# A two-layer encoder with 32 experts on one core: the first expert's two blocks by halves of its rows, the buffer refilled by halves, a pick moved behind them, and six added products ahead of the ranks

## The reference, cut to what matters

```
def route(xt, w_router, router_bias):
    scores = sigmoid(xt @ w_router); biased = scores + router_bias
    g_sel = argmax(sum of the 2 highest biased scores of each group)
    masked = where(in_group(g_sel), biased, -inf)
    _, idx = lax.top_k(masked, 2)
    w = take_along_axis(scores, idx); return idx, w / sum(w)

def expert(xb, e):                       # 32 experts, each for the tokens that chose it
    g, u = split(xb @ w_gu[e], 2, axis=-1)
    return (silu(g) * u) @ w_dn[e]

for i in range(2):
    x = x + g1 * mixer[i](modulate(x, norm_mix[i], sh1, sc1))
    h = modulate(x, norm_ffn[i], sh2, sc2)
    x = x + g2 * sum over k of w[:, k] * expert(h, idx[:, k])
```

## Time and profile before

| | |
|---|---|
| median of 3 runs | 1720.48 us (1718.47 to 1720.78) |
| profiled execution, its own time | 1716.08 us |
| its span, first to last instruction | 1714.3 us |
| mean granted TensorE clock | 0.904 |
| PE busy | 1363.5 us, 80% |
| DVE, ACT, POOL busy | 40%, 21%, 17% |
| moved by DMA | 517.29 MB, mean 302 GB/s |
| the chain that ended last | PE 50%, DMA 37%, DVE 8% |

### The profile page before, as it was taken

The page is one execution under the profiler, slowest core; times in us unless marked ns, Lnnn a source line. Parts: engine busy times, 40 slices in busy tenths (PEclk is TensorE's granted clock), DMA queues, the critical chain, the costliest instruction groups (busy, mean ns, idle before and its releaser), DMA issues.

```text
span 1714.3 us, 33172 instructions
## 1 busy us (share of the span) xinstructions
PE 1363.5 (80%) x14067; PEld 742.5 (43%) x14067; DVE 688.5 (40%) x1322; ACT 356.2 (21%) x717; POOL 298.8 (17%) x340
## 2 busy tenths in 40 slices
PE   3999899898956758797746999797986767698854
PEld 3644455444534334364424444344543334364432
DVE  5676677667311102121205378656531112022113
ACT  3345565221100001010002144523110001011000
POOL 1001122000312122132100122200131123122200
PEclk9998999998978879899977999898997889899987
DMA  9651422499999999999997122047799999999997
GB/s 367 242 217 69 164 75 77 142 321 404 380 391 401 406 387 386 405 389 410 412 417 286 49 74 74 24 171 320 290 397 397 405 405 386 402 389 401 420 426 292
DMA packets 66841, 517.29 MB, mean 302 GB/s; under 512 B 13277, under 2 KB 26102, under 8 KB 49034
## 3 DMA queue, kind: packets, MB, share of 16 engines
q1 hardware_dynamic: 51696, 493.77, 72.7%
q0 software_dynamic: 10848, 16.24, 2.8%
q10 hardware_dynamic: 4154, 5.18, 0.9%
HBM read 506.27 MB, written 22.04 MB: 308 GB/s over the span
## 4 chain that ended last, share of the span: by engine, by line
PE 50%; DMA 37%; DVE 8%; ACT 2%; issue 2%; SPq 1%; PEldq 1%; POOL 0%; ACTq 0%; DVEq 0%; POOLq 0%
DMA ring_gu<-in_moe_w_gu_dram 31%; PE ps L1188 15%; PE ps L1195 6%; PE ps L1078 6%; DMA ring_gu<-in_w_ada_dram 4%; PE ps L1113 3%; PE ps L995 3%; PE ps L1097 2%; PE ps L908 2%; PE ps L969 2%; PE ps L1015 2%; PE ps L888 2%; DMA arena<-xn_dram,tok_idx 2%; PE ps L1137 2%; PE ps L935 2%
## 5 line engine op out<-in xcount | busy, mean ns | idle before, releaser
L1188 PE MATMUL ps<-ring_gu,arena 128*32 128x256 f32 x5248 | 350.5, 423 | 173.6 <-DMA ring_gu<-in_moe_w_gu_dram 159.2
L1188 PEld LDWEIGHTS ps<-ring_gu,arena 128*32 128x32 f32 x5248 | 182.7, 121 | 323.2 <-issue 124.4
L2087 DVE TENSOR_TENSOR arena<-arena,ps 128x128 f32<-128x128 f32 x120 | 34.5, 287 | 631.5 <-ACT arena L1611 631.4
L719 POOL DMA_INDIRECT ys_dram<-arena,out_idx x116 | 114.7, 989 | 659.8 <-DVE arena L2081 618.8
L1611 ACT ACTIVATE arena<-ps 128x128 f32<-128x128 f32 x120 | 33.3, 278 | 886.8 <-PE ps L1188 886.8
L1188 PE MATMUL ps<-arena 128*32 128x256 f32 x2432 | 153.5, 409 | 61.5 <-DMA arena<-in_moe_w_gu_dram 58.3
L1195 PE MATMUL ps<-ring_dn,arena 128*32 128x256 f32 x2624 | 155.9, 379 | 2.8 <-DVE arena L2092 2.8
L712 POOL DMA_INDIRECT arena<-xn_dram,tok_idx x104 | 95.8, 922 | 278.4 <-issue 151.3
L1188 PEld LDWEIGHTS ps<-arena 128*32 128x32 f32 x2432 | 81.9, 118 | 127.2 <-DMA arena<-in_moe_w_gu_dram 53.5
L1195 PEld LDWEIGHTS ps<-ring_dn,arena 128*32 128x32 f32 x2624 | 84.4, 110 | 61.3 <-DVE arena L2092 3.7
L1078 PE MATMUL ps<-arena 128*128 128x512 f32 x256 | 110.6, 592 | 0.2 <-ACT arena L1325 0.2
(11 more groups left out here) (360 smaller groups left out, 1551.9 us busy)
## 6 DMA issues: line engine op xcount, KB each, us to landing
ring_gu<-in_moe_w_gu_dram SPq DMA_DIRECT2D x44, 4096.0 KB, 31.8
ring_dn<-in_moe_w_dn_dram SPq DMA_DIRECT2D x43, 2048.0 KB, 28.8
arena<-in_moe_w_gu_dram SPq DMA_DIRECT2D x18, 4096.0 KB
arena<-in_moe_w_dn_dram SPq DMA_DIRECT2D x20, 2048.0 KB, 28.8
ring_gu<-in_w_ada_dram SPq DMA_DIRECT2D x12, 2048.0 KB, 20.3
ring_gu<-in_w_ada_dram SPq DMA_DIRECT2D x48, 512.0 KB, 4.9
ring_gu<-ys_dram SPq DMA_DIRECT2D x8, 1024.0 KB, 9.5
arena<-in_rnn_w_in_dram SPq DMA_DIRECT2D x8, 1024.0 KB, 6.9
```

The costliest lines, as they stand in the source:

```text
L719: g.indirect_dma_start(ys_dram, bass.IndirectOffsetOnAxis(ap=out_idx[:, col:col + 1], axis=0), yo[:, n % 4, :], None, bounds_check=2 * TIL ...
L1188: last = mm(ps[s_ * ROWS:(s_ + 1) * ROWS, pb, 0:2 * QF].rearrange("p (a b) -> p a b", a=2), rows[:, k, :], pair[:, :, s_, :], start=(k == ...
```

## The change

Four edits.

1. Blocks 0 and 1, PE. Before, block 0's eight steps were followed by block 1's eight. Now the first four steps of block 0, the first four of block 1 (then the new semaphore `gu_half`), the last four of block 0, the last four of block 1. The down product of block 0 follows as before.
2. The load of place 3 (expert 3 into the buffer of expert 0), SP. Before, one DMA of 4 MB after block 1's product. Now two of 2 MB: the first half of each partition's row after `gu_half`, the second after block 1's product. `gu_landed` counts the additional 16.
3. `pick_rows(1, 0)` on PE moves from before block 0 to after block 2 and the down product of block 1; its copy `picks_out(1, 0)` on ACT moves from before block 0's Silu to before block 3's.
4. Ahead of the wait for `chosen_ready`, PE makes `KEEP_BUSY` = 6 products of 128x512 from `ident` and `x_tok` into the bank that the ranks overwrite. Nothing reads them.

A fifth edit: the semaphore `mrow_in` is merged into `rows_in` at the kernel's start.

```
@@ -473,7 +474,8 @@
         def gu_landed(place, l):
-            return landed(place, l) + (16 * (FT + l) if place % RING == RING - 1 else 0)
+            pieces = {0: l + (place >= RING), 1: 0, RING - 1: FT + l}
+            return landed(place, l) + 16 * pieces[place % RING]
@@ -585,8 +587,13 @@
                 def load_expert(n):
                     o = ORDER[n]
                     e = o if n < FIXED else sp.value_load(order_i[o:o + 1, 0:1], min_val=0, max_val=NE - 1)
+                    rows = GU[n % RING].rearrange("p k n -> p (k n)")
+                    half = KT * HALF if n == RING else 0
+                    if half:
+                        sp.wait_ge(S["gu_half"], l + 1)
+                        sp.dma_start(rows[:, 0:half], gu_rows(l, e)[:, 0:half]).then_inc(S["gu_in0"], 16)
                     sp.wait_ge(S["gu_done"], gone(n - RING, l))
-                    sp.dma_start(GU[n % RING].rearrange("p k n -> p (k n)"), gu_rows(l, e)).then_inc(S[f"gu_in{n % RING}"], 16)
+                    sp.dma_start(rows[:, half:KT * D], gu_rows(l, e)[:, half:KT * D]).then_inc(S[f"gu_in{n % RING}"], 16)
                     sp.wait_ge(S["dn_done"], gone(n - RING, l))
@@ -1116,8 +1122,11 @@
+                g = STAGES[f"rank{l}"]
+                pe.wait_ge(*emptied(before_in_bank(g + 1)))
+                for _n in range(KEEP_BUSY):
+                    mm(bank(g + 1), ident[:, :], x_tok[:, 0, 0:HALF], start=True, stop=True)
                 pe.wait_ge(S["chosen_ready"], l + 1)
-                g = STAGES[f"rank{l}"]
@@ -1153,7 +1162,6 @@
                 picks_transposed(0)
-                pick_rows(1, 0)
@@ -1248,7 +1256,13 @@
                     mine_rows = xgT[:, t % 2, :, q * ROWS:(q + 1) * ROWS]
-                    gate_up(2 + n % 2, mine_rows, GU[place % RING], range(KT // 2))
+                    if n > 1:
+                        gate_up(2 + n % 2, mine_rows, GU[place % RING], range(KT // 2))
+                    if n == 0:
+                        gate_up(2, mine_rows, GU[0], range(KT // 2))
+                        if base:
+                            pe.wait_ge(S["hmid_ready"], base)
+                        gate_up(3, xgT[:, 0, :, ROWS:2 * ROWS], GU[0], range(KT // 2)).then_inc(S["gu_half"], 1)
                     if q == TILES - 2 and t and t + 1 < NU:
                         rows_transposed(t + 1)
                     gate_up(2 + n % 2, mine_rows, GU[place % RING], range(KT // 2, KT)).then_inc(S["gu_done"], 1)
@@ -1257,6 +1271,8 @@
                     if not block_first(n):
                         block_down(n - 1)
+                    if n == 2:
+                        pick_rows(1, 0)
@@ -1564,7 +1580,6 @@
                 rows_out(0)
-                picks_out(1, 0)
@@ -1598,6 +1613,8 @@
+                    if n == TILES - 1:
+                        picks_out(1, 0)
                     if n == TILES:
                         picks_out(1, 1)
```

More of the change, by code:

```diff
@@ L46 @@
 GROUP = 4
+KEEP_BUSY = 6
 SKIP = 1 << 20
@@ L383, in trunk @@
         for name in (
-                "x_in", "c_in", "rows_in", "misc_in", "brow_in", "gate_biased", "pool_const", "mrow_set", "mrow_in", "c_ready", "ada_in0", "ada_in1",
+                "x_in", "c_in", "rows_in", "misc_in", "brow_in", "gate_biased", "pool_const", "mrow_set", "gu_half", "c_ready", "ada_in0", "ada_in1",
                 "ada_in2", "ada_in3", "cols_made", "ffn_in", "more_pe", "more_pool",
@@ L778, in _ @@
             pe.wait_ge(S["pool_const"], 1)
-            pe.wait_ge(S["rows_in"], 16 * 9)
+            pe.wait_ge(S["rows_in"], 16 * 13)
             pe.wait_ge(S["brow_in"], 16)
-            pe.wait_ge(S["mrow_in"], 16 * 4)
             g = STAGES["setup"]
```

8 lines of the change are left out of this document (4 added, 4 removed).

## The result

The changed kernel took 1724.28 us (median of 14 runs, 1718.78 to 1729.75), the kernel before 1718.33 us in the same comparison (14 runs, 1713.04 to 1722.05). The ratio is 1.0030, with a 95% interval of 1.0018 to 1.0043: some 5 us slower, where 3.6 us less was predicted. In the trace after, layer 1 begins 3.17 us later: the router's last product starts at 1180.07, and before it was

A forecast was written before the change was run, and what follows sets the result against it. Expert stages were taken as DMA-bound, with PE's chain having slack up to place 5. Gains of 2.7 us (layer 1) and 0.7 (layer 0) made 3.4, stated as 3.6: 1720.5 - 3.6 = 1716.9 us, range 1713.3 to 1720.8.

The forecast's parts named there:

- the halves and the six products: Layer 1: first half of place 3 issued 6.7 us earlier; six products make ranks and picks 3.1 us faster.
- the bare gap and its clock: PE ahead of block 0: about 2 us idle, clock falls to half, costing blocks 0 and 1 1.6 us.
- PE's slack is then 3.3 us: Layer 1, place 5: DMA finishes places 3 and 4 after PE's issue, so PE may run 3.3 us later.
- slack 3.5 us: Layer 0, place 5: the same margin of PE before DMA work ends, 3.5 us.
- Most of the 6.7 us is given back: Layer 1: place 3's earlier start is mostly lost in stream gaps between places 3, 4 and 5; 2.7 us gained.
- + 0.6 and + 2.8: PE chain's lateness at place 5, us: layer 1 2.1 + 1.6 - 3.1, layer 0 2.1 + 1.6 - 0.9.
- the chain at place 5 in layer 1: Layer 1: PE's chain 0.6 us late, place 5 issued at 1241.5 and moving at 1242.6.
- the six in layer 0: Layer 0: ranks start 1.9 us late, then ranks 1.0 and picks 1.8 us faster; net 0.9 us early.
- C: Rival, layer 1: the six don't hold the clock over ranks and picks; only layer 0 gains 0.7; 1719.8 us; chance 0.20.
- E: Rival, layer 0: the six run at half rate, PE's chain 8.0 us late; 1725.0 us; chance 0.09.
- The prediction's D: Rival, place 3's load: the added DMA costs 1.1 us per layer, 2.2 in all; 1719.1 us; chance 0.04.
- The last case in the list of what would make it wrong: A gain spent at a later wait of PE, such as the gathers of units 2 and 3; no size given.

The follow-up runs named there:

- e4: Kernel before with only unit 0's second pick moved behind block 2, in both layers; ratio to before 1.0030 (1.0018 to 1.0042).
- e9: Kernel before with the pick moved behind block 2 in layer 1 alone; ratio to before 1.0025 (1.0011 to 1.0039).
- e5: Kernel before run again unchanged, giving its second profile; ratio to before 0.9994 (0.9980 to 1.0008).
- e2: Kernel before with only the six products added ahead of the ranks; ratio to before 1.0002 (0.9986 to 1.0019).
- e7: Kernel before with halves and half load in both layers, six products in layer 1 only, pick not moved; ratio to before 0.9992 (0.9975 to 1.0009).
- e3: Kernel before with only the halves of blocks 0 and 1 and place 3's half load; ratio to before 1.0012 (0.9999 to 1.0026).
- e8: Kernel before with eight added products (3.45 us) on PE between block 2's down products and block 3, both layers; ratio to before 1.0043 (1.0025 to 1.0062).
- e11: Kernel before with all gathers of units 2 to 14 as plain transfers of fixed rows; ratio to before 1.0261 (1.0245 to 1.0276).
- e12: Kernel before with gathers issued one by one behind the scatters instead of four in a row; ratio to before 1.0023 (1.0012 to 1.0035).
- e13: Kernel before with only unit 2's four gathers, in each layer, as plain transfers of fixed rows; ratio to before 0.9970 (0.9954 to 0.9986).
- e15: Kernel before with unit 0's scatters put off behind unit 1's transposes and block 4's products, nothing left out; ratio to before 0.9980 (0.9964 to 0.9995).

## Why the prediction was wrong, by its own steps

**Right in their moments, not in the gain: the halves and the six products.** The first half went 6.2 us earlier (6.7 foretold), place 3 in two pieces cost nothing on SP. The six in layer 1 ended as DVE's picks were ready (ranks at 1188.45, just where they were, with 0.19 us idle), the picks took 7.11 us for 9.43, foretold 7.0, and block 0 began at 1198.76 in the times of before, foretold 1198.7. In layer 0 the ranks began at 396.42, foretold 396.6. The gain built on these moments was not found: the halves alone are at 1.0012 (0.9999 to 1.0026), the six alone at 1.0002.

**Right: the bare gap and its clock.** 1.98 us bare ahead of block 0, foretold 2; blocks 0 and 1 took 8.80 us for 7.11, 1.7 us, foretold 1.6, at a granted 0.51. But it does not always fall: in layer 1 of e4 and e9 the same gap (1.98 and 1.97 us) left them at 7.11.

**Wrong: "PE's slack is then 3.3 us" and "slack 3.5 us".** This is the step that failed. It came from one execution in which PE needed 20.1 us from place 4 to place 5. In the second profile of the same kernel it needs 27.7, and DMA is through some 4 us before place 5 of layer 1 is issued. So PE was already the bound there, in layer 1 by some 4 us, and in layer 0 level with DMA, and "Most of the 6.7 us is given back", true as it is, stood beside a loss that the sum had set at nothing: the 2.1 us that the moved pick puts on the chain, and the clock's share, in each of two layers, 4.2 to 7.4 us in all. Measured: 5.2 for the pick alone, and 7.4 for 6.9 us of plain work at the same place. The size of the term was right: in layer 1 of e4, where the clock did not fall, place 4 comes 2.4 us later after the ranks than in e5, foretold 2.1. With no slack, the prediction's own chain terms, + 0.6 and + 2.8, give 3.4 us slower for the whole change; 5.2 were measured (3.1 to 7.4). In the profiles it is the stall that takes the slack (7.7 us between places 4 and 5 of layer 1, against 3.3); how POOL's transfers bring it about stays open.

**Mis-sized: the chain at place 5 in layer 1.** Foretold + 0.6; at place 4 it was + 1.1, at place 5 + 7.9, and the 6.8 us between are the stall, which the kernel before has too. Comparing with the first profile alone would have put all of it on the change.

**Mis-sized: the six in layer 0, foretold 0.9 us early.** The ranks and picks went as told, but behind the picks DVE waits for a stored row of xn_dram, which no step of the prediction named. PE's idle time ahead of unit 0's transposes is 0.97 us in the first profile of before and 2.06 in the second, and with the faster picks 4.17 (changed) and 5.53 (e2): what the picks save is waited for there. The wait is not the change's own, since DVE waits 4.15 us there in the second profile of before. In layer 1 the 3.3 us are in the profiles, and still e2 stands at 1.0002 and e7 at 0.9992; their intervals reach to 2.4 and 4.3 us of gain, so whether these 3 us are in the time stays open.

**The rivals.** C (1719.8) and E (slower by a half-rate clock in layer 0) did not happen as told. The prediction's D, 1.1 us a layer for the added DMA, is not seen on SP, and the interval of e3 leaves it open. The slower side had one mechanism with a chance of 0.09; that PE binds already was not among them. The last case in the list of what would make it wrong, a gain spent at a later wait of PE, came nearest.

## What to carry to other kernels

A slack is a difference of two long sums, and one profiled execution gives it without its spread: before a change spends it, read it from a second profile, or add a known piece of work at that place and time it, as e8 did. Where PE and a queue are near each other, work is best left in the gap in which PE waits anyway, even if that delays the first block. And when the kernel after shows something new, profile the kernel before again ahead of explaining it. Where gaps stand on one engine, look at the others in the same microseconds: here the late signals and the fallen clock cost more than the gaps on PE themselves.

## What the runs showed of the hardware

**Indirect transfers in a row on POOL held PE up, and its signals more than its products.** Each issue takes POOL 0.9 to 1.0 us with 0.3 between. In layer 1 of e5 the row begins at 1229.06, PE's work comes in pieces from 1233.9, some 5 us later; products still last their 0.38 us, and between them stand 0.2 to 0.8 us without a releaser. In the middle of unit 2 the pieces cost 3 us (down products from 1257.29 to 1262.4 us, which take 1.91 undisturbed). With plain gathers from the same queue at the same places there were none (e11), and with the gathers spread one by one behind the scatters 2 gaps for 33 on the down products (e12). What waited for PE's signals went on 1.5 to 1.8 us after the seventh transfer's end. It was in twelve of thirteen profiles in which unit 1 met the full row, and not in the first profile of before; in that one POOL issued the same row and PE ran on. What switches it is open. It is in the timed runs too, since removing it at one unit of each layer takes 3 to 5 us off (e13, e15).

The Trainium skill, "SBUF — State Buffer", section "SBUF: two separate sides", has it that PE never waits for another engine's port. The rows agree in so far as no product is longer in the stall (379 and 380 ns a product in e11 and e5); what is late is the next instruction, and the signal to the engines that wait. The Trainium skill, "Runtime: NRT & Kernel Launch", section "Instruction fetch mechanics", says that an engine fetches its instructions in blocks by a DMA queue of its own. That such a fetch is held up would fit gaps without a releaser, and no run here tried it. The traces speak against it: in layer 1 of e5 packets of the instruction queue start 36.5 and 57.2 us after the ranks, none between, and the pieces lie at 46 to 49. When the second one starts, PE has started 1013 products and weight loads since the ranks, in the first profile of before 1077 at the same packet, so PE had not used up more of what was fetched.

**A gather lands long after its issue.** In the first profile of before the 104 gathers have a median of 13.5 us from issue to landing. Spread over a unit instead of issued together, gathers made PE wait 121 us in 18 places (e12).
